# First token block's mixing and the output weights moved into the last ten projection units of a single-core hybrid trunk kernel

## The chip, the core and the metric

The kernel runs as one program on one core of a Trainium2 chip. The metric is the time of one execution in device microseconds (us). The core has TensorE for matrix products (PE in the profile, with PEld for its weight loads), VectorE (DVE), ScalarE (ACT), GpSimd (POOL) and SyncE (SP, which issues DMAs). Each engine works through its own queue in order; semaphores tie the queues together.

## The reference, cut to what matters

One layer: modulated RMSNorm, one input projection, three head groups, an output projection with residual, and a mixture of 16 experts. The change touches all up to the output projection.

```python
h = modulate(rmsnorm(x, norm1_w), m_lat[0], m_lat[1])      # 2048 tokens x 1024
hc = modulate(rmsnorm(xc, norm1_w), m_ctx[0], m_ctx[1])    # 256 context tokens
conf_u, q, k, v, af, ab, r, sc_u = split(h @ w_in)         # 2848 columns; k, v, af, ab also of hc
# per head g and pair of chunks: S_t = diag(a_t) S_(t-1) + k_t^T v_t, forward and backward
o_lat = o_within_chunks + q @ S_prev                       # 4 heads
y = concat([silu(layernorm(depthwise_conv(a * sigmoid(gate), 31 taps))),
            rms(o_lat) * gn_w * silu(r),
            bg * depthwise_conv(cg * xh, 3 taps)]) @ w_out
x = x + m_lat[2] * y                                       # then norm, router, experts
```

Every product that feeds the router is made as three fp32r products of high and low halves (`mm3`, lines 55 to 57).

## The kernel before, in words

Two functions share one block of five queues. `phase_project` makes the modulation, turns and modulates the tokens, and multiplies them with `w_in`. `phase_tail` mixes a block of 512 tokens at a time, splits it into high and low halves, and multiplies it with `w_out`. Routing and the experts follow after a barrier.

**Start.** POOL loads eight 1 MB pieces of `ada_w` (`adaw`, six buffers, L470). SP loads 13 small vectors (L397), the first weight tile (`weights(0)`, L322) and the tokens (`token_rows`, L382, six buffers `xb`). PE multiplies each `ada_w` piece (L899), DVE copies the result out (`ada_out`, L814). DVE also splits weight tile 0 (`split(0)`, L677) right after the third of these copies, and that split waits for ACT's half of it (L500), which waits for the load. Then PE turns token tiles (L917), ACT modulates them (L622), DVE splits them. Token buffers are reused: load i waits until all of group (i-6)//2 has been turned.

**Units.** The projection runs as 99 units of one weight tile (128 columns, `tiles`) by one area of 512 tokens (256 for the context). The first 15 units go area by area, the rest tile by tile. A unit is 24 matmuls, 8 for each line of `mm3`. Kinds of tile: `u`, `b` copied out; `g`, `a` conformer gate and value; `r` copied out by ACT through Silu (L519). The order of `tiles` puts short-conv tiles 3 to 5 and then the four `r` tiles last. PE's unit u needs bank u-3 to be read.

**Attention parts.** From unit 22 on, every third unit begins one of 20 parts (`begins`). ACT takes Abs, Exp and Ln for the decay (`logs`, L527 to L531), DVE sums them (`decays`), ACT makes exponentials (`exps`), DVE makes keys and queries (`keys`, ends with L780), PE makes `scores` (L979) two units later, DVE masks them (`masks`, L721), PE makes `outputs` (L999), which ACT copies out (L589). The last two parts begin at units 76 and 79.

**Convolution and recurrence.** DVE adds the 31 taps of the second conformer half (`tap`, L797) spread evenly over the units from `conv_start` to `conv_stop`. SP then stores the result, reads back the per-chunk updates into `state`, and DVE runs the recurrence (`step`, L805): 128 instructions, 32 for each head, heads in pairs, after the loop over units.

**Tail.** PE's steps `mix(n, k)` (k = 0 to 5) sum means and squares with a matrix of ones (L1215, L1222, L1241) and multiply queries with the state (`inter`, L1233). ACT takes squares, roots (L1323, L1326) and Silu (L1332), DVE the rest. The eight pieces of `w_out` are loaded by POOL into four buffers and split by ACT (`w_high`, L1307) and DVE (`w_low`, L1403), one after each step. Then ACT and DVE split the mixed tokens (`cat_hi` L1354, `cat_lo` L1480), and PE multiplies (`multiply`, L55 with output `by`). Blocks 1 to 3 are mixed between these products.

Of the kernel before, what the change touches and what calls it, by code (L numbers as in the profile page):

```python
# [12 lines left out]
F32R = mybir.dt.float32r  # L13
# [81 lines left out]
def phase_project(nc, v, sem, block, low, top):  # L95
# [4 lines left out]
             + [(OFF_SC + P * i, "u") for i in range(3)] + [(384, "g"), (128, "a")]  # L100
             + [(OFF_SC + P * i, "u") for i in range(3, 6)] + [(OFF_R + P * i, "r") for i in range(4)])
# [4 lines left out]
             + [(i, n) for i in range(NE_TILES, n_tiles) for n in range(5 if tiles[i][1] == "b" else 4)])  # L106
    NU, NEARLY = len(units), NE_TILES * len(AREAS)
    first = [units.index((i, 0)) for i in range(n_tiles)]
# [74 lines left out]
    conv_stop = [first[g_tiles[1]] + 1, first[a_tiles[1]] + 24]  # L183
# [3 lines left out]
    with ExitStack() as st:  # L187
        sb, ps = alloc(nc, st)
# [20 lines left out]
        def at(name, shape, offset, dt=F32):  # L209
# [21 lines left out]
        bank = [ps(f"bank{i}", [P, 512]) for i in range(NBANK)]  # L231
        zb, bvk, bu, bsf, bsb = (ps(n, [P, 512]) for n in ("zb", "bvk", "bu", "bsf", "bsb"))
# [21 lines left out]
                  "k_read": (S["k_read"], NJ), "o_read": (S["o_read"], 4 * HEADS)}  # L254
        v.forward, v.backward = [(s, NSTEP) for s in forward], [(s, NSTEP) for s in backward]
        v.stage_done = [(s, 16 * sum(x == i for x in slot_of.values())) for i, s in enumerate(stage_stored)]
# [57 lines left out]
        ]  # L314

        @block.sync
        def _(sp):
# [75 lines left out]

            sp.dma_start(crow[0:KD, :], by_row(v.c[0])).then_inc(S["c_loaded"], 16)
# [6 lines left out]
            sp.wait_ge(S["ada_multiplied"], NFIRST - 4)  # L401
# [5 lines left out]
            weights(2)  # L407
            sp.wait_ge(S["cleared"], 1)
# [3 lines left out]
            for i in range(6, 18):  # L412
                token_rows(i)
# [5 lines left out]
            for u in range(NSLOT):  # L419
# [16 lines left out]
                if u == conv_stop[1]:  # L436
# [4 lines left out]
                    for g in range(HEADS):  # L441
                        sp.dma_start(v.state[g][:, :, :], v.upd[g]).then_inc(state_loaded[g], 16)

        @block.gpsimd
        def _(pool):
# [21 lines left out]
            for b in range(NFIRST):  # L467
                if b >= 6:
                    pool.wait_ge(S["ada_multiplied"], b - 5)
                pool.dma_start(adaw[b % 6][:, :, :], v.ada_w[0, :, b * 256:(b + 1) * 256].rearrange("(k p) n -> p k n", p=P)  # L470
                               ).then_inc(ada_loaded[b % 6], 16)
# [18 lines left out]
            if NSLOT - 1 in slot_of:  # L490
                store(NSLOT - 1)

        @block.scalar
        def _(act):
# [157 lines left out]
            for u in range(NSLOT):  # L652
# [15 lines left out]
                if u in split_at:  # L668
                    split(split_at[u])

        @block.vector
        def _(dve):
# [127 lines left out]
            def step(g, k):  # L800

                for half, over, c, of in ((F, forward[g], k + 1, k), (B, backward[g], NSTEP - k, NSTEP - k + 1)):
                    if k:
                        dve.wait_ge(over, k)
                    nc.vector.scalar_tensor_tensor(v.state[g][half, c, :], v.state[g][half, of, :],  # L805
                                                   v.pair_decay[half, g, c:c + 1], v.state[g][half, c, :],
                                                   ALU.mult, ALU.add).then_inc(over, 1)

# [49 lines left out]
            for u in range(NSLOT):  # L858
# [1422 lines left out]
```

## Time and profile before

| what | value |
| --- | --- |
| three timed runs | 2257.66 us median (2257.53 to 2260.46) |
| profiled execution | 2258.45 us, of it 2256.7 us span |
| PE busy over the span | 2127.7 us (94%) |
| DVE busy | 1386.1 us (61%) |
| ACT busy | 970.7 us (43%) |
| mean granted TensorE clock | 0.968 of full |

In the page's 40 slices (56.4 us each) PE is below 9 tenths in slice 1 (start), slices 13 and 14 (end of the projection and start of the tail) and slices 19 and 20 (routing). Matmul ends are modelled, so a busy PE is not a PE at its peak; where the span matters, the idle time before an instruction and what released it say more than the share.

### The profile page before, as it was taken

Reading aid. Unit: us, or ns where it says so; the run is one execution under the profiler, and the core shown is the slowest. Engines: PE = TensorE matmul, PEld = TensorE weight load, DVE = VectorE, ACT = ScalarE, POOL = GpSimd, SP = SyncE. Lnnn points to the kernel's source line nnn. Section 1 sums busy time; section 2 is a strip of 40 time slices with the busy share of each in tenths; the row PEclk is TensorE's granted clock in tenths of the full one; section 3 lists DMA queues with packets and bytes.
Section 4 is the critical chain, followed back from the end, with each engine's and each line's share of the span. In section 5 each row is a group of like instructions: output and inputs, shape, how many; then the busy total and the mean of one; then the engine's idle time right before and its main releaser. Section 6 shows DMA issues by size and latency. Waiting matters only on the chain. (4 is left out here: it accounts for less than half of the span.)

```text
span 2256.7 us, 34676 instructions
## 1 busy us (share of the span) xinstructions
PE 2127.7 (94%) x13430; PEld 1852.3 (82%) x13430; DVE 1386.1 (61%) x2106; ACT 970.7 (43%) x1594; POOL 289.6 (13%) x350
## 2 busy tenths in 40 slices
PE   6999999999998599994799999999999999999995
PEld 3778888787886388883699999999999999999994
DVE  2564537995968576656556565565555655556656
ACT  3922444344411444431244444444444444444445
POOL 1000000000001010010101221111211112112120
PEclk9999999999999699996799999999999999999997
DMA  6463333333334654436366565666556655657555
GB/s 250 135 235 128 109 102 95 121 123 91 118 117 149 239 200 164 140 122 240 127 242 206 197 212 185 244 207 220 187 203 225 233 198 187 217 207 259 197 185 227
DMA packets 182171, 408.45 MB, mean 181 GB/s; under 512 B 15988, under 2 KB 44980, under 8 KB 181188
## 3 DMA queue, kind: packets, MB, share of 16 engines
q1 hardware_dynamic: 153684, 309.97, 39.2%
q0 software_dynamic: 28400, 97.30, 13.3%
q8 instruction: 56, 0.92, 0.2%
q14 instruction: 31, 0.25, 0.0%
HBM read 329.98 MB, written 77.25 MB: 180 GB/s over the span
## 5 line engine op out<-in xcount | busy, mean ns | idle before, releaser
L55 PE MATMUL bh<-xt_hi,shi 128*128 128x256 f32 x2048 | 580.5, 283 | 3.2 <-DVE slo L2088 3.2
L56 PE MATMUL bh<-xt_lo,shi 128*128 128x256 f32 x2048 | 580.3, 283 | 0.0
L57 PE MATMUL bh<-xt_hi,slo 128*128 128x256 f32 x2048 | 580.2, 283 | 0.0
L2088 DVE TENSOR_TENSOR slo<-raw,shi 128x1024 fp32r<-128x1024 f32 x384 | 455.8, 1222 | 162.4 <-ACT shi L2006 159.3
L2006 ACT ACTIVATE shi<-raw 128x1024 fp32r<-128x1024 f32 x384 | 388.9, 1050 | 127.2 <-PE eby L57 127.2
L55 PEld LDWEIGHTS bh<-xt_hi,shi 128*128 128x128 f32 x2048 | 393.9, 192 | 4.3 <-issue 3.7
L56 PEld LDWEIGHTS bh<-xt_lo,shi 128*128 128x128 f32 x2048 | 394.0, 192 | 0.6
L57 PEld LDWEIGHTS bh<-xt_hi,slo 128*128 128x128 f32 x2048 | 393.9, 192 | 0.0
L55 PE MATMUL bank<-h_hi,whi 128*128 128x512 f32 x704 | 284.2, 404 | 0.0
L56 PE MATMUL bank<-h_lo,whi 128*128 128x512 f32 x704 | 278.1, 395 | 0.0
L57 PE MATMUL bank<-h_hi,wlo 128*128 128x512 f32 x704 | 277.9, 395 | 0.0
L55 PE MATMUL eby<-shi,ht_hi 128*128 128x512 f32 x512 | 204.6, 400 | 6.9 <-DVE slo L2088 6.9
L2010 ACT ACTIVATE sil<-bh 128x256 f32<-128x256 f32 x128 | 49.2, 384 | 358.7 <-PE bh L57 358.6
L56 PE MATMUL eby<-slo,ht_hi 128*128 128x512 f32 x512 | 201.2, 393 | 0.0
L57 PE MATMUL eby<-shi,ht_lo 128*128 128x512 f32 x512 | 201.1, 393 | 0.0
L2093 DVE TENSOR_TENSOR hft<-sil,bh 128x256 f32<-128x256 f32 x128 | 53.9, 421 | 211.5 <-ACT sil L2010 211.5
L57 PEld LDWEIGHTS bank<-h_hi,wlo 128*128 128x128 f32 x704 | 132.0, 187 | 32.2
L55 PEld LDWEIGHTS bank<-h_hi,whi 128*128 128x128 f32 x704 | 132.2, 188 | 29.4 <-ACT stage L519 0.3
L56 PEld LDWEIGHTS bank<-h_lo,whi 128*128 128x128 f32 x704 | 132.3, 188 | 28.7
L519 ACT ACTIVATE stage<-bank 128x512 f32<-128x512 f32 (+3 forms) x83 | 48.1, 579 | 240.7 <-PE bank L57 237.7
L1894 POOL TENSOR_TENSOR epause<-epause 128x1 f32<-128x1 f32 x60 | 38.6, 643 | 866.0 <-DVE gidx L2109 478.0
L797 DVE SCALAR_TENSOR_TENSOR acc<-zbuf,vcol,acc 128x1568 f32<-128x1568 f32 (+14 forms) x60 | 125.0, 2083 | 1.4
(341 smaller groups left out, 3232.4 us busy)
## 6 DMA issues: line engine op xcount, KB each, us to landing
raw<-in_exp_w_dram SPq DMA_DIRECT2D x96, 2048.0 KB, 11.2
uT<-stage POOLq DMA_DIRECT2D x72, 256.0 KB, 2.5
xb<-in_ada_w_dram SPq DMA_DIRECT2D x24, 512.0 KB, 5.5
wraw<-in_w_in_dram SPq DMA_DIRECT2D x22, 512.0 KB, 4.8
adaw<-in_ada_w_dram POOLq DMA_DIRECT2D x8, 1024.0 KB, 13.1
xb<-in_x_dram SPq DMA_DIRECT2D x16, 512.0 KB, 4.6
xt<-in_x_dram POOLq DMA_DIRECT2D x16, 512.0 KB, 4.9
x2d<-xt POOLq DMA_DIRECT2D x16, 512.0 KB, 2.9
```

The lines of the kernel that those rows point to most:

```text
L55: nc.tensor.matmul(out, w_hi, x_hi, start=start, stop=False)
L56: nc.tensor.matmul(out, w_hi, x_lo, start=False, stop=False)
L57: return nc.tensor.matmul(out, w_lo, x_hi, start=False, stop=stop)
L519: nc.scalar.activation(stage[slot_of[u]][0:m, 0:w], src, ACT.Silu if kind == "r" else ACT.Copy).then_inc(S["act_read"], 1)
L797: nc.vector.scalar_tensor_tensor(a3[:, :, lo:hi], z3[:, :, lo + s:hi + s], wcol, a3[:, :, lo:hi], ALU.mult, ALU.add).then_inc(S["tap_added ...
L1894: pool.tensor_tensor(pause[:, 1:2], pause[:, 0:1], pause[:, 0:1], ALU.add).then_inc(S["carried"], 1)
L2006: nc.scalar.activation(item_dst(shi, n), item_src(n), ACT.Copy).then_inc(S["w_hi_ready"], 1)
L2010: nc.scalar.activation(sil[f % 2][:, :], bh[f % 2][:, 0:CAP], ACT.Silu).then_inc(S["silu_ready"], 1)
L2088: nc.vector.tensor_tensor(item_dst(slo, n), item_src(n), item_dst(shi, n), ALU.subtract).then_inc(S["w_lo_ready"], 1)
L2093: nc.vector.tensor_tensor(hft[f % 2][:, :], sil[f % 2][:, :], bh[f % 2][:, CAP:2 * CAP], ALU.mult).then_inc(S["hidden_ready"], 1)
```

## The change

1. `tail_stage` no longer opens its own program part. Its steps are functions, and `phase_project` calls `sync_ahead`, `pool_ahead`, `tensor_ahead`, `scalar_ahead` and `vector_ahead` at the end of each unit's turn, with r = u - 91. PE's steps 0 to 5 of block 0 stand behind units 94 to 98 and in turn 99; the other engines' likewise. Its banks and buffers are placed in areas of the projected tokens that the last units have done with.
2. The last two tiles are now short-conv tiles 4 and 5, and their eight units go area by area. The four `r` tiles stand before them, at units 75 to 90 (before: 83 to 98).
3. The taps end three units earlier. The recurrence goes head by head, 16 instructions at each of the turns 89 to 96.
4. `w_out` comes in two loads of 2 MB, at turns 95 and 97, each to four `w_high` and `w_low`.
5. `ada_w` is loaded by SP, ahead of the vectors. `split(0)` stands behind the sixth `ada_out`. Tokens 6 to 9 are loaded ahead of the decay weights and `weights(3)`.

```diff
-             + [(OFF_SC + P * i, "u") for i in range(3)] + [(384, "g"), (128, "a")]
-             + [(OFF_SC + P * i, "u") for i in range(3, 6)] + [(OFF_R + P * i, "r") for i in range(4)])
+             + [(OFF_SC + P * i, "u") for i in range(3)] + [(384, "g"), (128, "a"), (OFF_SC + P * 3, "u")]
+             + [(OFF_R + P * i, "r") for i in range(4)] + [(OFF_SC + P * i, "u") for i in (4, 5)])
...
+             + [(i, n) for i in range(NE_TILES, n_tiles - 2) for n in range(5 if tiles[i][1] == "b" else 4)]
+             + [(i, n) for n in range(4) for i in (n_tiles - 2, n_tiles - 1)])
+    LAST = NU - 8
...
-    conv_stop = [first[g_tiles[1]] + 1, first[a_tiles[1]] + 24]
+    conv_stop = [first[g_tiles[1]] + 1, LAST - 3]
...
+            for b in range(6):
+                modulation(b)
             for dst, src in vectors:
                 sp.dma_start(dst, src).then_inc(S["vectors_loaded"], 16)
             weights(0)
             token_rows(0)
             token_rows(1)
-            sp.wait_ge(S["ada_multiplied"], NFIRST - 4)
+            modulation(6)
+            modulation(7)
             token_rows(2)
...
             weights(2)
+            for i in range(6, 10):
+                token_rows(i)
             sp.wait_ge(S["cleared"], 1)
             gate_weights(0)
             gate_weights(1)
             weights(3)
-            for i in range(6, 18):
+            for i in range(10, 18):
                 token_rows(i)
...
-                if b == 2:
+                if b == 5:
                     split(0)
...
                 if u in split_at:
                     split(split_at[u])
+                if LAST - 2 <= u < LAST + 6:
+                    if u == LAST - 2:
+                        wait_exps(dve, NJ - 1, "fac")
+                    g, k = divmod(u - LAST + 2, 2)
+                    if k == 0:
+                        dve.wait_ge(state_loaded[g], 16)
+                    for k in range(8 * k, 8 * k + 8):
+                        step(dve, g, k)
+                tail.vector_ahead(dve, u - LAST)
             assert done == [CONF_K, CONF_K]
-            wait_exps(dve, NJ - 1, "fac")
-            for pair in ((0, 1), (2, 3)):
-                for g in pair:
-                    dve.wait_ge(state_loaded[g], 16)
-                for k in range(NSTEP):
-                    for g in pair:
-                        step(g, k)
...
+        def sync_ahead(sp, r):
+            if r == 2:
+                done(sp, "area2")
+                block_in(sp, 0)
+                query_in(sp, 0)
+                query_in(sp, 1)
+                stages_done(sp, 2)
+                gate_in(sp, 0)
+                gate_in(sp, 1)
+            if r == 4:
+                stages_done(sp, 4)
+                short_in(sp, 0)
+            if r == 5:
+                query_in(sp, 2)
+                short_in(sp, 1)
+            if r == 6:
+                query_in(sp, 3)
...
+            if r in (4, 6):
+                done(pool, f"area{r}")
+                i = r // 2 - 2
+                pool.dma_start(raw[i][:, :, :], v.w_out[0, 4 * i * P:4 * (i + 1) * P, :].rearrange("(k p) n -> p k n", p=P)
+                               ).then_inc(S[f"w_loaded{i}"], 16)
...
+        def tensor_ahead(pe, r):
+            if r == 3:
+                done(pe, "u_read", "k_read", "o_read")
+                pe.wait_ge(S["ones_set"], 1)
+            if 3 <= r < 9:
+                pe_mix(pe, 0, r - 3)
...
+        def scalar_ahead(act, r):
+            if r == 3:
                 nc.scalar.preload_act_table_set("natural_log_exp_and_others")
+            if 3 <= r < 9:
+                act_mix(act, 0, r - 3)
+            if 6 <= r < 9:
+                w_high(act, 2 * (r - 6))
+                w_high(act, 2 * (r - 6) + 1)
...
+        def vector_ahead(dve, r):
+            if 3 <= r < 9:
+                dve_mix(dve, 0, r - 3)
+            if 6 <= r < 9:
+                w_low(dve, 2 * (r - 6))
+                w_low(dve, 2 * (r - 6) + 1)
```

ACT's queue at the part that begins at unit 79 (`ke`: decay logarithms, `stage`: a unit's copy, `whi`: a split weight tile). Before:

```order
L519 ACTIVATE stage<-bank 128x512 x2
L570 ACTIVATE ktok<-bvk 128x512
L576 ACTIVATE pt<-bsf 128x512
L527 ACTIVATE ke<-zb 128x512
L529 ACTIVATE ke<-ke 128x512
L531 ACTIVATE ke<-ke 128x512
L500 ACTIVATE whi<-wraw 128x1024
L519 ACTIVATE stage<-bank 128x512
L545 ACTIVATE ke<-ke 128x512
```

After, at the same part:

```order
L539 ACTIVATE stage<-bank 128x512 x2
L590 ACTIVATE ktok<-bank 128x512
L596 ACTIVATE pt<-bank 128x512
L547 ACTIVATE ke<-bank 128x512
L549 ACT_TABLE_LOAD
L549 ACTIVATE ke<-ke 128x512
L551 ACT_TABLE_LOAD
L551 ACTIVATE ke<-ke 128x512
L520 ACTIVATE whi<-wraw 128x1024
L539 ACT_TABLE_LOAD
L539 ACTIVATE stage<-bank 128x512
L565 ACT_TABLE_LOAD
```

The copies between the parts' steps are now Silu copies, so a table load stands ahead of Exp, of Ln and of the copy. The part that begins at unit 76 has the same loads.

DVE's queue at the end of the taps (`acc`) and the recurrence (`state`, numbered by head). Before:

```order
L797 SCALAR_TENSOR_TENSOR acc<-zbuf,vcol,acc 128x32x49
L677 TENSOR_TENSOR wlo<-wraw,whi 128x1024
L805 SCALAR_TENSOR_TENSOR state_50<-state_50,pair_decay 64x128 x2
L805 SCALAR_TENSOR_TENSOR state_51<-state_51,pair_decay 64x128 x2
L805 SCALAR_TENSOR_TENSOR state_50<-state_50,pair_decay 64x128 x2
L805 SCALAR_TENSOR_TENSOR state_51<-state_51,pair_decay 64x128 x2
```

After (`cat` is block 0's mixed tokens, `scuf` its short-conv input):

```order
L818 SCALAR_TENSOR_TENSOR acc<-zbuf,vcol,acc 128x32x49
L698 TENSOR_TENSOR wlo<-wraw,whi 128x1024
L326 SCALAR_TENSOR_TENSOR state_88<-state_88,pair_decay 64x128 x32
L698 TENSOR_TENSOR wlo<-wraw,whi 128x1024
L326 SCALAR_TENSOR_TENSOR state_89<-state_89,pair_decay 64x128 x32
L326 SCALAR_TENSOR_TENSOR state_90<-state_90,pair_decay 64x128 x32
L326 SCALAR_TENSOR_TENSOR state_91<-state_91,pair_decay 64x128 x16
L1466 SCALAR_TENSOR_TENSOR cat_50<-bank,cat_50 128x1024
L1474 TENSOR_TENSOR cat_50<-cat_50,bank 128x512
L326 SCALAR_TENSOR_TENSOR state_91<-state_91,pair_decay 64x128 x16
L1474 TENSOR_TENSOR cat_50<-cat_50,bank 128x512
L1510 TENSOR_TENSOR scuf<-scuf 128x513
```

The first head's recurrence now stands ahead of the last weight split, and 80 instructions of the other heads stand between that split and the block's first centring and addition.

SP's queue in the start. Before:

```order
L382 DMA xb_69<-in_x_dram 128x1024
L382 DMA xb_70<-in_x_dram 128x1024
L322 DMA wraw_64<-in_w_in_dram 128x8x128
L330 DMA wab<-in_gla_wa_f_dram 16x64
L332 DMA wab<-in_gla_ba_f_dram 1x64
L330 DMA wab<-in_gla_wa_b_dram 16x64
L332 DMA wab<-in_gla_ba_b_dram 1x64
```

After:

```order
L411 DMA adaw_93<-in_ada_w_dram 128x8x256
L396 DMA xb_105<-in_x_dram 128x1024
L396 DMA xb_106<-in_x_dram 128x1024
L336 DMA wraw<-in_w_in_dram 128x8x128
L396 DMA xb_107<-in_x_dram 128x1024
L396 DMA xb_108<-in_x_dram 128x1024
L336 DMA wraw_102<-in_w_in_dram 128x8x128
L396 DMA xb_103<-in_x_dram 128x1024
L396 DMA xb_104<-in_x_dram 128x1024
L396 DMA xb_105<-in_x_dram 128x1024
L396 DMA xb_106<-in_x_dram 128x1024
L344 DMA wab<-in_gla_wa_f_dram 16x64
```

The last `ada_w` piece now goes ahead of tokens 2 and 3 in the same queue, and tokens 6 to 9 go ahead of the decay weights.

## Rows read from the trace of the kernel before

**Rows 1.** Stage windows: length, busy of each engine (count), PEclk, DMA share, GB/s
```profile
112.80:724.30 611.50, 611.15 (x3462) 491.34 (x3459) 421.90 (x610) 228.62 (x465) 49.69 (x90) 1.00 0.38 124
724.30:775.90 51.60, 20.61 (x49) 10.59 (x49) 33.62 (x51) 24.63 (x31) 6.03 (x12) 0.60 0.80 276
```

**Rows 2.** Waits, first 45 us: who for whom, total us, times, longest
```profile
PEld bvk L907 <- DVE mrow L814: 7.1, 1, 7.1
```

**Rows 3.** Timeline of the start: start, us, what [idle before it <- releaser]
```profile
33.91 1.93 PE L899 MATMUL bank<-adaw,swide 128*32 128x256 f32 x16
...
34.80 1.06 ACT L594 ACTIVATE junk<-xb 128x1024 f32<-128x1024 f32 x1
...
39.76 0.56 ACT L622 ACTIVATE hf<-zb,shift,scale 128x256 f32<-128x256 f32 x1 [1.02 <-PE zb L917]
```

**Rows 4.** Window of the DMA-bound start, columns as in Rows 1
```profile
4.00:37.00 33.00, 21.97 (x158) 11.62 (x158) 4.77 (x14) 8.54 (x16) 7.44 (x16) 1.00 1.03 386
```

**Rows 5.** Timeline around ACT's wait for tokens 6 and 7
```profile
44.24 0.69 PE L917 MATMUL bsf<-ident,xb 128*128 128x128 f32 x2 [0.18 <-ACT hf L622]
...
51.82 18.66 SPq L382 DMA_DIRECT2D xb<-in_x_dram  x6
...
56.61 1.06 ACT L594 ACTIVATE junk<-xb 128x1024 f32<-128x1024 f32 x1 [6.18 <-DMA xb<-in_x_dram]
```

**Rows 6.** Timeline, the parts of units 76 and 79 on DVE
```profile
584.80 0.69 DVE L731 SCALAR_TENSOR_TENSOR ke<-zb,ke 128x512 f32<-128x512 f32 x1 [0.33 <-ACT ke L531]
...
606.24 0.76 DVE L721 COPY_PREDICATED pt<-m_up,bsb 128x512 f32<-128x512 int32 x1 [1.01 <-ACT pt L576]
...
614.22 2.28 DVE L797 SCALAR_TENSOR_TENSOR acc<-zbuf,vcol,acc 128x1984 f32<-128x1984 f32 x1
...
620.27 0.69 DVE L780 TENSOR_TENSOR q<-bs,fac_q 128x512 f32<-128x512 f32 x1
...
628.44 0.75 DVE L721 COPY_PREDICATED pt<-m_up,bsb 128x512 f32<-128x512 int32 x1 [0.57 <-ACT pt L576]
```

**Rows 7.** The same parts: PE's last scores and ACT's copy of outputs
```profile
624.04 0.32 PE L979 MATMUL bsf<-q,kc 64*128 64x64 f32 x1
...
634.71 0.60 ACT L589 ACTIVATE ost<-bsf 128x512 f32<-128x512 f32 x1 [0.29 <-PE bsf L999]
```

**Rows 8.** The tile `state`: recurrence, ns min/median/max; its four loads' landing
```profile
L805 DVE SCALAR_TENSOR_TENSOR state<-state,pair_decay x128: 339/348/354, 682.2 to 730.4; 64x128 f32<-64x128 f32 x128
...
DMA to landing us min/median/max: 5.2/9.6/13.8
```

**Rows 9.** Timeline: convolution store, last weight split, recurrence
```profile
667.57 0.34 SPq L377 DMA_DIRECT2D accT<-acc  x1
...
681.09 1.22 DVE L677 TENSOR_TENSOR wlo<-wraw,whi 128x1024 fp32r<-128x1024 f32 x1 [13.55 <-ACT whi L500]
682.23 48.54 DVE L805 SCALAR_TENSOR_TENSOR state<-state,pair_decay 64x128 f32<-64x128 f32 x128
```

**Rows 10.** Timeline: last unit's copy, first sums, centring
```profile
724.31 0.60 ACT L519 ACTIVATE stage<-bank 128x512 f32<-128x512 f32 x1 [5.00 <-PE bank L57]
...
730.97 3.72 PE L1215 MATMUL bm<-cat,ones 128*128 128x512 f32 x4 [6.69 <-POOL ones L1196]
...
739.69 1.22 DVE L1409 SCALAR_TENSOR_TENSOR cat<-bm,cat 128x1024 f32<-128x1024 f32 x1
```

**Rows 11.** Timeline: last root, table load, weights, first product
```profile
765.72 0.69 ACT L1323 ACTIVATE rs<-bn,epsc 128x512 f32<-128x512 f32 x1 [0.62 <-PE bn L1241]
...
769.92 1.28 ACT L1334 ACT_TABLE_LOAD   x1
771.21 2.00 ACT L1307 ACTIVATE wo_hi<-h 128x1024 fp32r<-128x1024 f32 x2
...
775.85 0.80 PE L55 MATMUL by<-wo_hi,ct_hi 128*128 128x512 f32 x1 [10.17 <-DVE ct_lo L1480]
...
784.57 1.05 PE L1233 MATMUL bi<-qp,state 128*128 128x128 f32 x8
```

More of the change, by code:

```diff
@@ L314, in phase_project, with step @@
         ]
+        def step(dve, g, k):
+            for half, over, c, of in ((F, forward[g], k + 1, k), (B, backward[g], NSTEP - k, NSTEP - k + 1)):
+                if k:
+                    dve.wait_ge(over, k)
+                nc.vector.scalar_tensor_tensor(v.state[g][half, c, :], v.state[g][half, of, :],
+                                         v.pair_decay[half, g, c:c + 1], v.state[g][half, c, :],
+                                         ALU.mult, ALU.add).then_inc(over, 1)
         @block.sync
@@ L669, in _ @@
                     split(split_at[u])
+                tail.scalar_ahead(act, u - LAST)
         @block.vector
@@ L1043, in _, with tail_stage @@
                         outputs(begins[u - 3])
-def phase_tail(nc, v, sem, block, low, high):
+                tail.tensor_ahead(pe, u - LAST)
+def tail_stage(nc, v, sem, low, high):
     NBK, TILES = L // NB, NB // P
@@ new lines, in pe_mean, with pe_spread @@
+        def pe_mean(pe, n):
+            pe.wait_ge(S["conv_loaded"], 32 * (n + 1))
+            wait(pe, "log_ready", 5 * (n - 1) + 1)
+            for ch in range(2):
+                last = nc.tensor.matmul(bm[:, :], ones[:, :], cat[n % 2][:, ch, :], start=(ch == 0), stop=(ch == 1))
+            last.then_inc(S["mean_ready"], 1)
+        def pe_spread(pe, n):
+            pe.wait_ge(S["centred"], n + 1)
+            for ch in range(2):
+                pe.wait_ge(S["squares_ready"], 6 * n + ch + 1)
+                nc.tensor.matmul(bm[:, :], ones[:, :], sq[ch][:, :], start=(ch == 0), stop=(ch == 1)
+                                 ).then_inc(S["squares_summed"], 1)
@@ new lines, in pe_inter @@
+        def pe_inter(pe, i):
+            n, h = divmod(i, HEADS)
+            if n == 0:
+                pe.wait_ge(*v.forward[h])
+                pe.wait_ge(*v.backward[h])
+            pe.wait_ge(S[f"query_loaded{i % 2}"], 16 * (i // 2 + 1))
+            wait(pe, "added", i)
+            for j in range(TILES):
+                last = nc.tensor.matmul(bi[:, j * P:(j + 1) * P], v.state[h][:, TILES * n + j + 1, :],
+                                        qp[i % 2][:, j * P:(j + 1) * P], start=True, stop=True)
+            last.then_inc(S["inter_ready"], 1)
@@ L2237, in trunk_kernel @@
                 v.hc_hi, v.hc_lo = csb("hc_hi", [P, KD, LC], F32R), csb("hc_lo", [P, KD, LC], F32R)
-            with nc.Block() as block:
-                phase_project(nc, v, sem, block, low, high)
-                phase_tail(nc, v, sem, block, low, high)
+            with ExitStack() as pst, nc.Block() as block:
+                _, ps = alloc(nc, pst)
+                v.bank = [ps(f"bank{i}", [P, 512]) for i in range(8)]
+                tail = tail_stage(nc, v, sem, low, high)
+                phase_project(nc, v, sem, block, low, high, tail)
+                tail.emit(block)
         stage_over()
```

507 lines of the change are left out of this document (245 added, 262 removed).

## The prediction

> **What bounds the kernel now.** I read the page's slices first, then windows over stages, then the waits and the timeline at each place where PE stands idle. Three stretches matter.
>
> From 112.8 to 724.3 PE is busy 611.15 of 611.50 us [rows 1]. So nothing on other engines costs time there, and whatever the start gains is carried to the projection's end unless PE is made to wait.
>
> The start is bound by loads. From 4 to 37 us the DMA engines are full and move 386 GB/s [rows 4]. PE's weight loads wait 7.1 us for one copy by DVE [rows 2], which was queued behind the split of weight tile 0. Later ACT waits 6.18 us for tokens 6 and 7, which SP issued at 51.82, although the turn that frees their buffers had ended at 44.9 [rows 5]: SP stood at `weights(3)`.
>
> The largest hole is the step into the tail. Between 724.30 and 775.90 PE is busy 20.61 of 51.60 us at a mean granted clock of 0.60 [rows 1]. First the recurrence holds DVE until 730.8 [rows 9]; then mixing and weight splits alternate until 775.85 [rows 11].
>
> I give times on the axis of before. A shift of the start moves all that follows alike.
>
> **Start, first part.** What moves: eight `ada_w` loads from POOL to SP, past 13 small vectors, weight tile 0 and (the last two) tokens 0 and 1; `split(0)` behind the sixth copy. In SP's order 9.63 MB (eight times 1.05, two times 0.52, and 0.19 of small ones) have to land before PE's last `ada_w` product. At 386 GB/s [rows 4] that is 24.9 us. Traffic is full at 4.0; SP can issue at 1.6, right behind its first two rows, so I let it begin at 3.5: 28.4 against 33.91 [rows 3], 5.5 earlier. The 7.1 us wait lies inside this and is not counted again. Late next are tokens 2 and 3, now queued behind those pieces: 1.05 MB, 2.7 us, so 31.1. Before, ACT's square of token tile 3 began at 34.80 and the first modulation at 39.76, 1.02 of it idle [rows 3]; 31.1 + 3.9 = 35.0. Gain 4.8. Bounds: 1 if one queue moves 1 KB pieces at 330 GB/s instead of 386 (9.63 MB would take 29.2 us, and 1.05 MB 3.2), 7 if the wait of 7.1 goes whole. POOL loses only issues; its memsets come earlier and nobody waits.
>
> The Trainium skill speaks against the first move: "DMA: Bandwidth & Descriptors", section "Issuing engines are not separate DMA queues", says that DMAs of all issuing engines run on the same 16 engines, and another issuer saves only issue time. By that rule SP in place of POOL gives nothing, and the gain is that of order alone. The trace agrees that the engines are full, with 386 GB/s.
>
> **Start, second part.** Tokens 6 to 9 go ahead of the decay weights and `weights(3)`. Issued at 44.9 in place of 51.82, with the same 4.8 us to landing, they are there at 49.7; ACT arrives at 50.4 [rows 5]. The whole 6.2 goes; bounds 3 and 6.5. Each later token load waits for a turn that moves along, so I add no new wait. `weights(3)` comes some microseconds later, hidden by units of the first tiles. Start together: 11.0 earlier.
>
> **Table loads and taps in the last two parts.** The four `r` tiles now meet the parts of units 76 and 79. ACT gets two table loads in the logarithms and one each before the Silu copies and the exponentials. A load is 1.28 us and the next instruction starts 0.01 later [rows 11]. The logarithm's two are on DVE's path, the others hide in ACT's waits. Taps run two a turn in place of 1.6: one more at turns 74, 77, 80 and 82, 2.0 to 2.3 each [rows 6].
> - Unit 76: the tap of turn 74 is absorbed, the logarithm is 2.56 late, so decays start 2.6 late (584.80 before), keys 4.7 late with the tap. The masks, 1.01 idle before, come 3.7 late.
> - Unit 79: decays 3.4 late, keys with the third tap 5.6 late. Before, the product that `scores` needs was done when L780 could start, 620.27; now 625.9. PE arrives at 624.04 [rows 7]: it waits 1.9.
> - The next masks, 0.57 idle before [rows 6], end at 637.1; PE wants them at 633.8 (ACT's copy of the outputs at 634.71 less 0.9 [rows 7]) plus 1.9: it waits 1.4.
>
> Together +3.3. Bounds 0 and 8. The same skill, "ScalarE: Activation LUTs", section "What ACT_TABLE_LOAD costs", gives about 2.66 us for each switch, a drain included; by that this term would be about 4 us larger. No drain shows in [rows 11].
>
> **The last ten units.** Anchor A is the end of the last weight split, 682.23 before [rows 9]; it waits for unit 90, so it stands fixed to PE. The taps end near 656.6 (637.1, nine taps of about 2.0, one split) against 667.57. Storing and reading back as before, the first state lands near 667 [rows 8, 9], so head 0's 32 steps (12.1 us) are done before A. Behind A stand 80 steps of 48.54 / 128 = 0.379 [rows 9], 30.3 us, then centring and addition, 1.8 [rows 10]: A+32.1.
> - PE: units are 5.6 apart (0.60 + 5.00 [rows 10]) and unit 98 ended at A+42.1, so unit 94 ends at A+19.7. Mean and first `inter` take 1.7 and 0.8 at full clock (3.72 at half [rows 10]; 1.05 less overlap [rows 11]), unit 95 ends at A+27.8. The second `inter` waits for the addition until A+32.1: a new wait of 4.3. Queued behind it are three units; behind ACT's squares, the copies of units 95 on.
> - Two sums of squares until A+34.4. In the hole of 724.3 the clock falls, so I add 1.5 for products at half clock after this wait. Units 96, 97 and 98 with their `inter` and norm (1.7 each) and 1 us for query 3, which SP issues behind short-conv loads that wait for DVE, end at A+57.1; two norms, A+58.9. The last root waits for two weight splits on ACT (2.00 [rows 11]) and a root before it: A+61.3.
> - From the last root to the first product the instructions are those of before: 775.85 - 765.72 = 10.1 [rows 11]. First product at A+71.4, in place of 775.85 = A+93.6. Gain 22.2. Bounds 12 and 29.
>
> What hides the rest: steps, short-conv, weight splits of DVE and ACT lie beside 24-matmul units. If they don't fit, PE waits in its own projection. `w_out`'s second 2 MB starts near A+44 and has 15 us. Behind the first product nothing is changed: blocks 1 to 3 have their loads by then (gates of block 0 done about 5 us ahead).
>
> **Sum.** -4.8 - 6.2 + 3.3 - 22.2 = -29.9. Against the profiled execution, 2258.45 (1.75 over its span): 2228.55. The median of the runs is 0.8 lower: 2227.8. I forecast 2228.
>
> **Rivals.**
> - *No wait in the projection.* The part lag is absorbed and DVE is ahead at the second `inter`: 3.3 + 4.3 + 1.5 less, 2219. For it: every lag above rests on slack of 1 to 4 us. Against: 80 steps behind A are countable.
> - *The start is a matter of bandwidth.* Order helps little, since 386 GB/s is full anyway: first part 1, second 3, so 7 less gain, 2235. This is the skill's rule taken whole. For it: [rows 4]. Against: the 7.1 us wait was not one for bytes.
> - *The mixing costs PE more.* In-order queues: PE's banks wait for ACT's copies, which stand behind squares and roots that wait for PE. Two further waits of 4 to 5 us: 2237.
> - *Slower: the recurrence paces everything.* In place of four chains, only two alternate, so a step waits for one only a single instruction ahead. At 0.348 long and 0.379 apart [rows 8, 9] that fits now. If a step took 0.76, 80 steps would add 30.5 and the 16 after them 6, which gives 2228 + 36.5 = 2264. It decides from about 0.69 us a step. Against: one step's length covers the other's result.
>
> **How the numbers follow.** Chances: forecast 0.51 (2222 to 2232), no wait 0.14, bandwidth 0.14, more waits 0.16, slower 0.04, no difference 0.01. The range takes the cases up to the third rival and the term bounds: 2217 to 2241. Below 0.2% (4.5 us) a measurement of this kernel can't tell a change. Faster 0.95, same 0.01, slower 0.04.
>
> **What would show it.** Right: the last `ada_w` product near 28, no 6 us wait of ACT for tokens 6, table loads at Exp, Ln and Silu, PE waits of 1 to 2 us at two places, one of 4 us after unit 95 for the addition, and 10 us from the last root to the first product. Wrong: a step cadence above 0.4, a last `ada_w` product after 31, or PE idle over 10 us in units 91 to 98. The forecast fails by more than its range if the hole after the last unit stays above 30 us or the clock stays low through those units.

## The result, and the profile of the changed kernel

The changed kernel takes 2236.04 us (median of four runs, 2234.92 to 2236.91). The kernel before takes 2258.54 on the same chip, and the ratio is 0.990, interval 0.988 to 0.991. It is 22.5 us faster. The forecast was 2228, 29.9 faster. The time alone stands nearer to two of the rivals (2235 and 2237) than to the forecast; which mechanism ran is read from the trace. Profiled execution against profiled execution the gain is 2258.45 - 2236.91 = 21.5 us. Below, "after" is the changed kernel.

**The start.** First the timeline of PE and ACT (start, duration, engine, line, operation, then in brackets the idle time before and what ended it). It answers to [rows 3, 5].

```profile
29.97 1.94 PE L913 MATMUL bank<-adaw,swide 128*32 128x256 f32 x16 [6.44 <-DMA adaw<-in_ada_w_dram]
32.78 1.93 PE L913 MATMUL bank<-adaw,swide 128*32 128x256 f32 x16
...
35.28 1.06 ACT L614 ACTIVATE junk<-xb 128x1024 f32<-128x1024 f32 x1 [0.19 <-DMA xb<-in_x_dram]
39.12 0.55 ACT L642 ACTIVATE hf<-bank,shift,scale 128x256 f32<-128x256 f32 x1
```

DVE's split of weight tile 0 holds PE no longer, but PE now waits 6.44 us for the seventh piece of `ada_w`. The last product starts at 32.78 (33.91 before). ACT's square of token tile 3 starts at 35.28, as soon as the tile is there (34.80 before), and the first modulation at 39.12 (39.76 before). SP's issues and the load traffic (columns of the second: window and its length, POOL's busy time, PE's granted clock, DMA share, GB/s) say why:

```profile
1.63 10.62 SPq L411 DMA_DIRECT2D adaw<-in_ada_w_dram  x6
18.64 0.42 SPq L336 DMA_DIRECT2D wraw<-in_w_in_dram  x1
21.13 1.56 SPq L411 DMA_DIRECT2D adaw<-in_ada_w_dram  x2
22.74 5.23 SPq L396 DMA_DIRECT2D xb<-in_x_dram  x2
```

```profile
16.00:18.50 2.50, 0.00 (x0) 1.00 1.09 385
18.50:21.00 2.50, 0.00 (x0) 1.00 1.12 265
21.00:24.00 3.00, 0.00 (x0) 1.00 0.90 272
24.00:28.00 4.00, 0.00 (x0) 1.00 0.94 312
```

The first six pieces take SP 10.6 us to issue: 0.4 for the first, up to 2.6 for a later one. The vectors and weight tile 0 follow (128 KB for 1024 rows, so 128 bytes each), and the DMA engines, still 90 to 112% busy, move only 265 to 312 GB/s until 28 us, where [rows 4] had 386 over the whole start (here the same 33 us have 358).

ACT's wait of 6.18 for tokens 6 and 7 [rows 5] is gone. The first copy of a unit comes at 57.86 (64.88 in the trace of before, where this row wasn't shown), and units up to 560 us run 7.1 earlier. So the start gave 7.1 us: 0.6 at the first modulation, 6.4 at the tokens.

**The parts of units 76 and 79** (PE's waits between 590 and 800 us: total, times, longest):

```profile
PE bank L55 <- DVE ct_lo L1545: 11.5, 1, 11.5
PE bank L1277 <- DVE cat L1474: 4.5, 1, 4.5
PE bank L993 <- DVE bs L798: 1.7, 1, 1.7
PE bank L1285 <- ACT rs L1372: 1.0, 1, 1.0
PE bank L1013 <- DVE pt L745: 0.2, 1, 0.2
```

The third and fifth rows are the new waits in the parts. Behind the first of them PE runs at its lower level for some products (mean granted clock 0.98 between 560 and 640; 1.00 over the same 80 us before). The last weight split ends at A = 678.86, against 682.23 [rows 9]: 3.7 of the 7.1 us are spent. How they are spent differs between profiles. Three runs below leave this stretch as it is in after (`s_pieces_on_pool`, `s_pieces_together`, `t_steps_early`), and there the clock holds at 1.00 between 615 and 630. Their two waits are 1.6 and 1.2, and the last split comes 3.5 to 3.7 us late all the same, counted from the first copy of a unit. In `u_steps_ahead` the clock falls for longer (0.77 between 615 and 630), and there it is 5.2. The waits of `s_pieces_on_pool`:

```profile
PE bank L989 <- DVE bs L794: 1.6, 1, 1.6
PE bank L1009 <- DVE pt L741: 1.3, 2, 1.2
```

**The last ten units and the step into the tail** (windows: PE busy, granted clock, DMA share, GB/s; this answers to the second stretch of [rows 1]):

```profile
678.90:706.00 27.10, 27.10 (x118) 1.00 0.57 188
706.00:710.50 4.50, 0.70 (x4) 0.94 0.98 385
710.50:738.00 27.50, 26.68 (x106) 0.89 0.45 154
738.00:751.50 13.50, 1.10 (x2) 0.72 0.78 244
```

Rows of DVE, ACT and PE, in order of time:

```profile
678.86 30.34 DVE L326 SCALAR_TENSOR_TENSOR state<-state,pair_decay 64x128 f32<-64x128 f32 x80
710.37 0.68 DVE L1474 TENSOR_TENSOR cat<-cat,bank 128x512 f32<-128x512 f32 x1
741.20 0.67 ACT L1372 ACTIVATE rs<-bank,epsc 128x512 f32<-128x512 f32 x1
751.52 0.77 PE L55 MATMUL bank<-wo_hi,ct_hi 128*128 128x512 f32 x1 [11.54 <-DVE ct_lo L1545]
760.18 0.69 DVE L1558 TENSOR_TENSOR h<-bank,mb 128x512 f32<-128x512 f32 x1 [8.91 <-PE bank L57]
```

The addition ends at A+32.2 after 80 steps of 0.379 us. The last root starts at A+62.3 and the first product at A+72.7, where it was A+93.6. The block is worth 21.0 us. Of the 51.6 us hole two are left: 4.5 us at the addition and 11.5 ahead of the first product.

Then 2.8 us are lost again. The first product is 24.3 us earlier than before, the first result (DVE L1558 above) 22.9, routing's first turn 22.05 (1036.39, now 1014.34), the end 21.5. 1.5 of them are lost in the first half product (24 matmuls, up to the next step's product), which takes 8.5 us here and 7.0 before: 14 products run 0.43 us apart until 757.6; before it was seven, until 778.6. This too scatters. In seven profiles with the same instructions from the last root to routing and the same wait of 11.5 us ahead, the half product takes 7.0 to 8.5 us (middle 7.6), and routing's first turn comes 260.5 to 262.8 us behind the first product (middle 262.3; 260.5 before). The profile of after is the longest of them: up to routing it loses 2.3 us, the middle one 1.7.

| step | forecast | measured |
|---|---|---|
| start, first part | -4.8 | -0.6 |
| start, second part | -6.2 | -6.4 |
| table loads and taps | +3.3 | +3.7 |
| last ten units | -22.2 | -21.0 |
| behind the first product (in this profile) | 0 | +2.8 |
| sum | -29.9 | -21.5 |

### The profile page after: what moved, and what is told of

Its sections match the earlier page's. It is cut to its first block and busy times, and to the rows that moved or that the text cites. A ratio compares the mean times of both kernels' runs of the same rounds, so it can differ in the third digit from the quotient of the medians.

```text
span 2235.2 us, 34681 instructions
## 1 busy us (share of the span) xinstructions
PE 2123.8 (95%) x13430; PEld 1851.6 (83%) x13430; DVE 1385.9 (62%) x2106; ACT 983.9 (44%) x1604; POOL 279.8 (13%) x336
```

## Experiments on the start

**The start alone**, in the kernel before.

```
-            for b in range(NFIRST): ...                 # POOL's eight loads
+            for b in range(6): modulation(b)            # SP, behind the two rows of c; (6), (7) ahead of tokens 2 and 3
-                if b == 2: split(0)                     # DVE
+                if b == 5: split(0)
+            for i in range(6, 10): token_rows(i)        # SP, ahead of gate_weights(0)
```

> The kernel before with both edits of the start and nothing else (ada_w's eight pieces on SP behind the first two rows, split(0) behind the sixth copy, tokens 6 to 9 ahead of the decay weights). If the parts of the change add up, it takes over what the trace of after shows for its start and no more: 7.1 us from the before of the same runs, of which 0.6 to 0.7 shows at the first modulation (39.1) and the rest where ACT waited 6.18 for tokens 6 and 7. The rival, that the start's gain in after hangs on the rest of the change, gives another number than 6.5 to 7.5 here. The prediction's own figure for this kernel was 11.0.

It takes 2251.37 (ratio to before 0.996, interval 0.995 to 0.998), 8.4 less than before; its span is 7.1 shorter. The 8.4 lie outside the 6.5 to 7.5 that were expected, but their interval (some 5 to 12 us) is too wide to decide. The trace is clearer: the first modulation is at 38.27, 1.5 earlier than in before, and the first copy of a unit at 57.01, 7.9 earlier, so the second part gives 6.4 without the rest of the change too. It also shows the scatter: seven profiles with this same start have their first modulation between 37.73 and 39.12, middle 38.27, so the profile of after is the latest of them and the first part is worth about 1.5, not 0.6.

**Pieces back on POOL.**

```
-            for b in range(6):
-                modulation(b)           # and modulation(6), (7) further on, on SP
+            sp.wait_ge(S["ada_multiplied"], NFIRST - 4)      # ahead of tokens 2 and 3
+            for b in range(NFIRST): ...  pool.dma_start(adaw[b % 6] ...)   # on POOL
```

> After with the eight ada_w pieces put back on POOL's queue and SP's wait for four products ahead of tokens 2 and 3 put back too; split(0) stays behind the sixth copy and tokens 6 to 9 stay early. My theory: putting split(0) later freed PE's products, and the move to SP took that gain away, because SP carries the pieces in 1 KB packets behind one another with the 128-byte packets of weight tile 0 in the same queue. Then here the products run at 2.8 us each, the last one starts near 29.5, the first modulation is near 35.5 in place of 39.12, and the kernel is 3 to 4 us faster than after (about 2232.5). The rival, bandwidth alone: the bytes are the same, so the first modulation stays between 38.5 and 39.8 and the time within 1 us of after.

```profile
26.27 0.42 ACT L516 ACTIVATE wa_hi<-wraw 128x256 fp32r<-128x256 f32 x1 [23.10 <-DMA wraw<-in_w_in_dram]
28.45 1.06 ACT L610 ACTIVATE junk<-xb 128x1024 f32<-128x1024 f32 x1 [1.76 <-DMA xb<-in_ctx_dram]
39.05 0.56 ACT L638 ACTIVATE hf<-bank,shift,scale 128x256 f32<-128x256 f32 x1 [0.36 <-PE bank L927]
```

My theory fell. Traffic is better here (398 to 416 GB/s between 16 and 30 us, as in before), and yet the first modulation is at 39.05 and the time 2237.02 (ratio 0.990), as the rival expected. With two queues the small loads and the context tokens share with the pieces: weight tile 0 lands only at 26.2, the last piece makes PE wait 1.83 us and its product starts at 33.19. The context tokens' square starts at 28.45 (24.61 in after), and from it to token tile 3's square, 6.3 us later, ACT never waits for a load. Neither queue wins. This is the Trainium skill's rule ("DMA: Bandwidth & Descriptors", section "Issuing engines are not separate DMA queues": all issuing engines' transfers run on the same 16 engines), and here the run agrees. It agrees for the big loads; the next run shows that the place of the small ones counts.

**Small loads on ACT.**

```
-            for dst, src in vectors: sp.dma_start(dst, src)...
-            weights(0)
+            for dst, src in vectors: act.dma_start(dst, src)...      # behind ACT's first Exp
+            act.dma_start(raw_of(0) ...)
```

> After with the 13 vectors and weight tile 0 issued by ACT behind its first exponential, so that they travel beside the pieces and not between the sixth and the seventh. My theory: the dip to 175-320 GB/s between 19 and 28 us is those small packets alone in the queue; beside large ones it goes, token tile 3 lands 2 to 3 us earlier (ACT's square at 32.5 to 33.3 in place of 35.28), and the kernel takes 2 to 3 us less than after. The rival, that the dip comes from the eight MB of 1 KB packets or from the memory itself: no window above 370 GB/s there, token tile 3 as before, no difference over 0.5 us.

```profile
18.50:21.00 2.50, 0.00 (x0) 0.50 1.10 402
21.00:24.00 3.00, 0.00 (x0) 0.50 1.03 399
24.00:28.00 4.00, 0.00 (x0) 0.50 1.09 383
```

```profile
32.54 1.06 ACT L611 ACTIVATE junk<-xb 128x1024 f32<-128x1024 f32 x1 [0.16 <-DMA xb<-in_x_dram]
36.38 0.55 ACT L639 ACTIVATE hf<-bank,shift,scale 128x256 f32<-128x256 f32 x1
```

The dip is gone, token tile 3 is 2.7 us earlier and so is the first modulation (1.9 against the middle of the seven). The same dip stands later, 276 GB/s between 24 and 28 us, in the next run, where the small loads come later. The time is 2232.40 (ratio 0.989), 3.6 below after's; the two ratios' intervals overlap, so it is the trace that decides. The same bytes go through the same engines; what costs is that small packets stood alone in a queue, with large ones waiting behind them. Whether the vectors or the 128-byte rows weigh more wasn't tried.

**All eight pieces together.**

```
-            for b in range(6):
+            for b in range(NFIRST):
                 modulation(b)                           # ahead of the vectors
```

> After with pieces 6 and 7 issued right behind the first six, ahead of the vectors, weight tile 0 and tokens 0 and 1. My theory: the first modulation is set by token tile 3, and all bytes ahead of that are the same, so although the last ada_w product starts 3 to 4 us earlier (29 in place of 32.78) the first modulation stays within 0.7 us of 39.12 and the time within 0.7 us of after. The rival, the prediction's own step (the last product and what follows it set the first modulation): 3 us faster.

```profile
27.11 1.93 PE L911 MATMUL bank<-adaw,swide 128*32 128x256 f32 x16
29.53 1.06 ACT L612 ACTIVATE junk<-xb 128x1024 f32<-128x1024 f32 x1 [0.73 <-DMA xb<-in_ctx_dram]
35.83 1.06 ACT L612 ACTIVATE junk<-xb 128x1024 f32<-128x1024 f32 x1
39.67 0.55 ACT L640 ACTIVATE hf<-bank,shift,scale 128x256 f32<-128x256 f32 x1
```

The last product is 5.7 us earlier, the first modulation 0.5 later (1.4 against the middle of the seven), the time 2236.35 (ratio 0.989). So the last product doesn't set the first modulation here. ACT does: in this run, in `s_small_on_act` and in all seven profiles with after's start the modulation comes 3.8 us behind the start of token tile 3's square. But what holds that square differs. In after it is the tile's load. Here it isn't: the context tokens are now behind all eight pieces and ACT gets to them 4.9 us later (29.53 against 24.61), and ACT runs from them to tile 3 without waiting for a load. The edit took one load off the path and put another on it.

## Experiments on the rest

**Table set ahead of the waits.**

```
+                if near_silu(...):       # an r tile in the last three units; first in logs and in exps
+                    nc.scalar.preload_act_table_set("natural_log_exp_and_others")
```

> After, with ACT loading the table set that holds both Exp and Ln ahead of the wait in the logarithms and in the exponentials of the parts that meet the r tiles. My theory (the prediction's third term, 3.3 forecast, 3.7 measured): the two loads of 1.28 us on DVE's path go, PE's waits for DVE near 625 and 633 (1.7 and 0.5) fall to under 1.0 together, and the units behind come 1.2 to 2.5 us earlier. The rival, that the taps carry the term (one more of about 2 us a turn at some turns): waits as before, under 0.5 us gained.

In after ACT runs, for one part's logarithms:

```profile
576.39 1.28 ACT L549 ACT_TABLE_LOAD   x1
...
578.34 1.28 ACT L551 ACT_TABLE_LOAD   x1
```

and here one load less, 2233.56 us (ratio 0.989). PE's waits are now:

```profile
PE bank L1021 <- DVE pt L753: 1.2, 1, 1.2
PE bank L1001 <- DVE bs L806: 1.0, 1, 1.0
```

Their sum is 2.2, not under 1.0 as expected. In after it is 1.9, but there the clock fell behind the first wait (0.50 between 622 and 624), and it is 1.00 here; L998's products of unit 82 (L1006 here) take 1.10 us in after and 0.68 here. Against the three profiles in which the clock held with the old tables, the first wait falls from 1.6 to 1.0, the second stays at 1.2, and the last split comes 1.1 to 1.3 us earlier, counted from the first copy of a unit. So one load of 1.28 was on the path and is gone, at the low end of what was expected. The rest of the two waits stays; DVE has the taps ahead of the masks (`pt`). What share the taps have wasn't tried by itself.

**16 steps earlier, first try.**

```
-        g, k = divmod(u - LAST + 2, 2)          # 8 k of one head a turn, turns LAST-2 .. LAST+5
+        lo, hi = (0, 8), (8, 24), then 8 a turn  # turns LAST-2 .. LAST+4
```

> After, with 16 of the 128 recurrence steps moved from behind the last weight split to ahead of it, where DVE waited 6.49 us. My theory: PE's wait of 4.5 us for the first addition goes (DVE adds at A+26.1 in place of A+32.1, PE wants it at A+27.8), the clock holds through units 96 to 98, and the first product starts 4.5 to 6 us earlier, near A+67.5. The rival, that ACT's squares and splits or query 3 set those units: PE waits elsewhere, the gain is under 2 us.

2233.33 us (ratio 0.989), and `PE bank L1279 <- DVE cat L1476` still 4.7. It is 2.7 below after's, and this profile starts 1.2 earlier for no reason in the edit. The edit missed: it took 16 steps from behind the addition and left 80 between the split and it.

**16 steps earlier, second try.**

```
+        lo, hi = ((0, 8), (8, 24), (24, 32), (32, 40), (40, 48), (48, 56), (0, 0), (56, 64))[u - LAST + 2]
```

> After, with 16 recurrence steps moved so that they are missing between the last weight split and the first addition: 16 more stand ahead of the split (where DVE waited), 64 in place of 80 between it and the addition, 16 behind as before. t_steps_early took the 16 from behind the addition, and the wait of 4.5 stayed (4.7), so it didn't test the wait. Theory: the wait is only DVE's count of steps; with 16 fewer (6.03 us) the addition ends at A+26.1 and PE's wait for it goes, the first product comes 4.5 to 6 us earlier (near A+67.5), and the kernel takes 2230 to 2231.5. The rival (ACT or loads set units 95 to 98): the wait reappears elsewhere, and it takes 2234 or more.

```profile
679.47 24.27 DVE L326 SCALAR_TENSOR_TENSOR state<-state,pair_decay 64x128 f32<-64x128 f32 x64
745.40 0.77 PE L55 MATMUL bank<-wo_hi,ct_hi 128*128 128x512 f32 x1 [11.54 <-DVE ct_lo L1547]
```

64 steps take 24.3 us, PE's wait for the addition is gone (0.5 for query 3 in its place), and the first product is at A+65.9, 6.7 us earlier than A+72.7. The granted clock is 1.00 from 706 to 712, where in after it was 0.50 from 711 to 715. The time is 2228.28 (ratio 0.986, interval 0.985 to 0.988), 7.8 below after's and below the 2230 to 2231.5 expected; in the profiles 2.3 us of the difference lie between the first product and routing, in the scatter told above. Wait and slow clock behind it cost more than the wait of 4.5 alone.

**Splits behind `ct_lo`.**

```
-            if 6 <= r < 9:                # turns LAST+6 .. LAST+8, w_high (ACT) and w_low (DVE)
+            if 6 <= r < 8:
             cat_hi(0)                     # and cat_lo(0) on DVE
+            for k in range(4, 8):
+                w_high(act, k)            # and w_low on DVE
```

> After, with the splits of w_out's last four rows on ACT and DVE (k 4 to 7) behind ct_hi and ct_lo in place of ahead of them. My theory: of the 10.1 us from the last root to the first product, 4.0 us of ACT and 2.4 to 4.7 us of DVE are splits that the first products do not need, so the first product starts 4 to 5.5 us earlier (PE's wait of 11.5 becomes 6 to 7.5), and the splits arrive in time. The rival, that PE then waits for w_lo inside its first half product: what is gained before is lost there, under 1.5 us net.

```profile
747.30 0.77 PE L55 MATMUL bank<-wo_hi,ct_hi 128*128 128x512 f32 x1 [8.10 <-DVE ct_lo L1545]
757.10 1.98 PE L1259 MATMUL bank<-cat,ones 128*128 128x512 f32 x4 [1.22 <-DMA cat<-accT]
```

The wait falls from 11.5 to 8.1, short of the 6 to 7.5 expected: a reload of the table set stood between the Silu and `ct_hi`. PE has its splits in time, but waits 1.2 for block 1's loads. Against its own start the first product is 3.6 us earlier, and that is still 3.2 at routing. The median, 2235.42 over runs from 2233.1 to 2238.6 (ratio 0.990), doesn't resolve it.

**The hole filled.**

```
+            for _ in range(40):
+                nc.tensor.matmul(bt[:, 0:P], v.ident[:, :], v.ident[:, :], start=True, stop=True)
```

> After, with 40 products of 128 columns on the identity, whose result nobody reads, on PE between the last norm and the first product, where it was idle for 11.5 us. My theory: the 2 to 3 us that after lost behind its first product are the clock (granted 0.50 until 757.6, 14 products of 0.43 apart; before only 7). With PE busy the clock is 1.00 at the first product, the first half product takes 5.6 us in place of 8.9, and the kernel is 2.5 to 3.5 us faster. The rival: the low clock is not due to idle time of PE there, and the half product takes 8 us or more again.

```profile
746.00:748.00 2.00, 1.44 (x13) 1.00 0.84 192
...
750.00:752.00 2.00, 2.00 (x5) 0.50 1.02 404
```

The filler ended 2.4 us before the product, and that was enough for the granted clock to fall to 0.50, PE's 1.2 GHz, for six products. The first half product takes 7.0 us, not 5.6, and that is inside the 7.0 to 8.5 of the profiles without a filler. So this run doesn't decide between theory and rival. It takes 2233.45 us (ratio 0.989), 2.6 below after's, and its profile starts 1.4 earlier for no reason in the edit.

**Together.** `v_best` joins small loads on ACT, pieces together, ACT's lookahead of one group in place of two, a table load behind each Silu of an `r` tile, the 16 steps, the splits and the reload behind `ct_lo`, and block 1's `cat` loads first. Of its lines that no run above has, these matter:

```
                 if kind == "r":
+                    nc.scalar.preload_act_table_set("natural_log_exp_and_others")
...
-            prepare(1)                    # and group g + 2 in the loop
+                if g + 1 < len(groups):   # group g + 1 in the loop
...
+            if n:                         # block 0 reloads the table set behind its last w_high instead
                 nc.scalar.preload_act_table_set("natural_log_exp_and_others")
...
+                if n == 1:
+                    block_in(sp, n)       # ahead of short_in and gate_in
```

> Five edits of after in one. Start: small loads on ACT, eight pieces of ada_w together, and ACT squares tokens 2 and 3 between the first modulations in place of ahead of them (group by group, one group ahead in place of two). Table set for Exp and Ln loaded right behind each Silu copy of the r tiles. 16 steps ahead of the split, as in u_steps_ahead. Splits of w_out's rows 4 to 7 and the reload of the table set behind ct_hi and ct_lo. Block 1's cat loads ahead of its short-conv and gate loads. By my theories: first modulation near 33.5 in place of 39.12, worth 4 to 5 us at the first units; tables 2 to 3; steps 4.5 to 6; splits and reload 4.5 to 5.5; DMA wait of 1.2 behind the first half product gone. Together 15 to 19 us less than after: 2217 to 2221. If the start stays bound by bytes, 3 less of it: up to 2224.

```profile
711.82 0.43 SPq L1167 DMA_DIRECT2D qp<-prep  x1
722.12 2.05 PE L1285 MATMUL bank<-qp,state 128*128 128x128 f32 x8 [5.93 <-DMA qp<-prep]
741.93 0.77 PE L55 MATMUL bank<-wo_hi,ct_hi 128*128 128x512 f32 x1 [6.96 <-DVE ct_lo L1555]
```

2228.24 us (ratio 0.986): no better than the steps alone, and outside the 2217 to 2224 expected. The first modulation is at 34.84, but a faster PE ran into a load: query 3, issued 711.82 behind the short-conv loads, took until 722.1. Behind this wait the granted clock is 0.50 until 726. One more edit, made on `v_best`:

```
                 query_in(sp, 2)
-                short_in(sp, 1)          # then query_in(sp, 3) a turn later
+                query_in(sp, 3)
+                short_in(sp, 1)
```

> v_best with one edit more: SP issues query 3 before the second short-conv loads, not behind them. In v_best PE waited 5.9 us for query 3: it was issued at 711.82, when the second 2 MB of w_out were under way, and landed at 722. The buffer is free once the second inter product has run (701.4). My theory: issued then, it is there before PE wants it (716.2), PE's wait of 5.9 goes whole, and the kernel takes 2221 to 2224. The rival, that what PE gains there it loses to w_out's load or to ACT's splits a unit later: 2226 or more.

```profile
733.40 0.76 PE L55 MATMUL bank<-wo_hi,ct_hi 128*128 128x512 f32 x1 [6.96 <-DVE ct_lo L1554]
```

2218.19 us (ratio to before 0.982, interval 0.980 to 0.983), 10 us less for one line moved, 17.9 less than after, and below the 2221 to 2224 expected. The expectation counted the wait of 5.9 alone; the first product comes 8.5 us earlier, because the slow clock behind the wait goes with it. The first product starts 18.1 us earlier than after's: 4.7 are the start and the parts, 13.4 lie behind the last weight split. This is the best version.

And with the same filler, 28 products long:

```
+            for _ in range(28):           # behind the last norm
+                nc.tensor.matmul(bt[:, 0:P], v.ident[:, :], v.ident[:, :], start=True, stop=True)
```

> v_best_query with 28 products on the identity (0.227 us each at full clock, 6.4 us; nobody reads the result) in the 7.0 us in which PE waits for the first ct_lo. In t_fill_hole the clock fell to 0.50 about 1.5 us after the filler ended, and rose again only 2.7 us after the first product; here the filler ends within 0.7 us of it. Theory (it is PE's idle time that brings the clock down): 1.00 through the first half product, 5.6 us in place of 8.3, and 2 to 2.7 us less than v_best_query. The rival (the clock falls there for another reason): the first half product takes 7 us or more, no difference over 0.5 us.

```profile
PE bank L1266 <- DMA cat<-accT: 2.2, 1, 2.2
PE bank L55 <- DVE ct_lo L1556: 0.5, 1, 0.5
```

```profile
736.00:738.00 2.00, 2.00 (x10) 1.00 0.99 357
...
744.00:746.00 2.00, 2.00 (x11) 0.50 1.04 399
```

The clock holds at 1.00, PE's 2.4 GHz, and the first half product takes 5.6 us (8.2 in `v_best_query`, and never under 7.0 in the profiles without a filler). So it is PE's idle time that brings the clock down there. And nothing is gained, 2218.79 (ratio 0.982): PE is through 2.5 us sooner, waits 2.2 for block 1's `accT` rows, and the clock falls in that wait. The loads are late next, and a filler doesn't bring them.

## Why the forecast held, and where it missed

The forecast range (2217 to 2241) held the time, and the mechanism was as described in three of the four steps that it priced. The range was wide, though: the time lies outside the forecast's own 2222 to 2232. And one of the prediction's own signs of being wrong came true, a last `ada_w` product after 31 (32.78).

- **Start, first part: this step failed** (forecast 4.8, bounds 1 to 7; measured 0.6, about 1.5 against the middle of seven profiles). The step as put: "At 386 GB/s [rows 4] that is 24.9 us", and then tokens 2 and 3 "1.05 MB, 2.7 us, so 31.1". It counted bytes and took the mean rate of a start in which small and large loads ran in two queues, for one in which they run in one. Token tile 3 came at 35.28. With the small loads beside the pieces it came at 32.54: 2.7 of the 4.2 us are these. The other 1.4 are loads from behind. By 31.0 us that run had moved the 10.7 MB that the forecast counts up to tile 3, as forecast (31.1); but the tile wasn't there until 32.5, and another 0.5 MB had been moved, by this count of loads issued behind it (columns: window and its length, POOL's busy time, PE's granted clock, DMA share, GB/s):

```profile
0.00:31.00 31.00, 2.91 (x18) 0.74 0.98 344
31.00:32.50 1.50, 0.00 (x0) 0.50 1.16 360
```

It isn't the last `ada_w` product (27.11 brought nothing), and POOL's queue in place of SP's gives nothing either. The rival "the start is a matter of bandwidth" had the size right for this part and wrong for the second (3 in place of 6.4). What the runs show is that order counts, and which loads share a queue.
- **Start, second part**: 6.2 forecast, 6.4 measured; ACT's wait went whole.
- **Table loads and taps**: +3.3, measured +3.7. The waits came where forecast, 1.7 and 0.2 in place of 1.9 and 1.4. Their sum is smaller than the term: the rest is products at the lower level behind the first wait, which the forecast left out. That the total fits isn't luck, since the three profiles in which the clock held show waits of 1.6 and 1.2 and nearly the same total; with a longer fall of the clock it can be 5.2 (`u_steps_ahead`). Of the loads, one of the logarithm's two is shown to be on the path (`t_table_early`), the taps' share isn't. Each load took 1.28 us with the next instruction 0.01 to 0.02 later; the larger figure of the Trainium skill ("ScalarE: Activation LUTs", section "What ACT_TABLE_LOAD costs", 2.66 with a drain) doesn't show in this trace.
- **Last ten units**: 22.2 forecast, 21.0 measured. The addition (A+32.1, measured A+32.2) and its wait (4.3, measured 4.5) came as worked out; the last root came at A+62.3 in place of A+61.3, and behind it the chain took 10.3 us in place of 10.1. The rival that more waits come was not needed; the one at ACT's root was 1.0.
- **The slower rival** needed 0.69 us a step; the step stayed at 0.379 with two chains in place of four.
- **Behind the first product**: 0 forecast, 2.8 measured in this profile, and about 1.7 up to routing in the middle of seven. "Behind the first product nothing is changed" was right of the instructions and wrong of the clock: in this profile 1.5 of it is the first half product, in the middle of the seven 0.6. That PE's idle time makes the clock is shown by the last run; where the rest goes wasn't tried.

## What to carry to other kernels

When a load moves to another queue, don't price it by bytes over the mean rate: ask which packets it will stand behind, and leave small ones a queue of their own beside the large. Count the work between an anchor and the instruction that PE waits for, and shorten that stretch only; the same 16 steps gave 1.4 us taken from behind it, 6.7 from inside it. Take the profiles of several runs with the same stretch before a difference of 1 us or 2 is given a cause. After each gain look up what is late next in the loads, since one line of order was worth 10 us once PE was faster.

## What the runs showed of the hardware

- Six loads of 1 MB took SP's queue 10.6 us to issue (0.4 the first, up to 2.6 a later one), the small vector behind them 2.5 and each of the next ones 0.3, and two token tiles 5.2 (4.7 and 0.5): issuing isn't cheap once much is under way.
- 128-byte rows and small vectors alone in one queue took the rate from 385 to between 265 and 312 GB/s with the engines over 90% busy; beside large loads of another queue the rate stayed at 383 to 402.
- After waits of 2.4 us (`t_fill_hole`) and 2.2 us (`v_best_filled`) PE ran its next products at 1.2 GHz, for 2.7 us in one case and about 4 in the other; after the wait of 0.5 it stayed at 2.4 GHz. A wait of 1.6 to 1.7 us was followed by 1.2 GHz in after (0.50 between 622 and 624) and not in `s_pieces_on_pool`, `s_pieces_together` and `t_steps_early`, so the length of the wait alone doesn't decide.
- The same instructions behind the same wait of 11.5 us took 7.0 to 8.5 us, according to how long the clock stayed at 1.2 GHz.
